# Hybrid attention and DeltaNet trunk: a quarter-size product in the second inversion level, and a later slot for layer 1's second query tile

## The chip, the cores and the metric

The kernel runs on one core of one Trainium2 chip. Its time is the device time of one execution in microseconds (us), as the median of the runs shown: 2465.13 us of 3 runs, from 2462.39 to 2465.59.

## The reference, cut to what matters

Two layers (DEPTH = 2) work on 512 tokens of 2048 channels: 256 context tokens and 256 latent ones. Each layer has one input projection, a mixer with two groups of 8 heads (group A is differential softmax attention, group B a bidirectional gated DeltaNet), and one output projection with an adaLN gate. Layer 1 doesn't update the context, so its attention has only latent queries. The parts that the change touches, shortened:

```python
def diff_attend(q, k, v, lam):                      # group A
    s = jnp.einsum('bhmqd,bhmkd->bhmqk', q, k) * (A_HEAD_DIM ** -0.5)
    p = jax.nn.softmax(s, axis=-1)
    a = p[:, :, 0] - lam * p[:, :, 1]
    return jnp.einsum('bhqk,bhkd->bhqd', a, v)

def gated_delta_chunked(q, k, v, g, beta, s0):      # group B, once forward, once flipped
    ...
    m = jnp.where(tri_strict, k_beta @ k.T * decay, 0.0) + jnp.eye(CHUNK)
    rhs = jnp.concatenate([v * beta[..., None], k_beta * jnp.exp(g)[..., None]], axis=-1)
    sol = lax.linalg.triangular_solve(m, rhs, left_side=True, lower=True, unit_diagonal=True)
    ...                                             # then a scan over the chunks
```

## The kernel before, in words

**Stages.** Each layer runs nine bodies, one after the other (`heads`). Body i projects head i's eight column tiles out of the 2048 channels and at the same time "fills" with the mixer of head i-1; body 0 only projects. The ninth (`project` is false) runs the mixer of head 7 beside the output projection. Body 0 of a layer, body 1 of layer 0 and the ninth are written out, the others run as a loop.

**Slots.** The order inside a body is written out by hand. It has 64 slots. Every engine (PE, DVE, ScalarE, and SP for the loads) builds a plan with `put(slot, function)` and then goes through the slots in order: first the slot's share of the projection, then the planned functions in the order in which they were put. On PE a slot of projection is six matmul rows of 128x512 (two k-tiles, each as hi x hi, L1808, hi weights x lo, L1809, lo weights x hi, L1810, since the float32 operands are split into a high and a low part); in layer 1 four of the eight tiles, the queries and the gates, are needed for the latent tokens alone and have half the width. On ScalarE a slot s with s % 4 = 1 begins with `split_hi` (L660, which waits for the weights' DMA), on DVE one with s % 4 = 2 with `split_lo` (L1113, `w_lo`). An engine that waits in a function holds up everything behind it on that engine.

**Solving the triangular system.** The kernel takes 128 tokens as one chunk (NT = 4 of them) and forms the inverse of the triangular matrix for both directions d, as `inv` and as its transpose `inv_T`. SP's `blocks_to_partitions` (L581 to L590) brings the 16x16 diagonal blocks onto partitions; DVE substitutes in four pieces (`substitute_backward`, slots 15 to 18 of layer 1, helpers at L296 and L312); SP's `blocks_back` (L592 to L601) stores the solution and issues eight DMAs (L600) that place the blocks into one of the two matrices; DVE's `turn_inv` (L1372, slots 24 and 25 of layer 1) transposes it into the other. Then the block size is doubled three times (`LEVELS = (16, 32, 64)`, so LVL = 3):
- levels n = 0 and 1, in layer 1 from slot 26 + 4n, in layer 0 from 23 + 4n, for each direction: `times_m` on PE (L1889, `m_T` x `inv` into bank GX[d]), `mask_x` on DVE (L1113 is the helper that records it, out of PSUM into `prod`), `times_inv` on PE (L1897 `inv_T` x `prod` into GX[d], L1898 `prod` x `inv_T` into GT[d], each for four chunks), and `merge` on DVE (two subtractions of 128x512, from `inv` and from `inv_T`; also recorded as L1113);
- the last level, the corners (slots 31 and 32 of layer 0, 34 and 35 of layer 1), in 64x64 pieces: `corner_times_m` (L1908) reads of `inv` only the quarter `QUAD[d]`, `copy_corners` (DVE, L1404), `corner_times_inv` (L1917) and `merge_corners` (two scalings of 64x256 out of PSUM, L1410). Behind it only `inv_T` is read (`v_mul`).

A float32 matmul has two rows in the trace for one call of `mm`, a 64x64 one too, so that four products stand as eight rows.

**Attention.** A query tile of 128 tokens goes through `score` on PE (L1985, 2 matmuls), `a_max` on DVE (L1470), `exps` on ScalarE (L929), `a_mix` on DVE (L1479 to L1482), `turn_p` on PE (L1992), `p_copy` on ScalarE (L941), `attend` on PE (L1999) and `oa_copy` on ScalarE (L946). Behind the last tile come `oa_squares` on ScalarE (L951), `oa_sums` on DVE (L1488), a power on POOL, `oa_norm` on DVE one slot ahead of `TURN_OA`, `turn_oa` on PE (L2005), and `y_out` on DVE and the store of y by ScalarE's DMA queue one and two slots behind it. `rotate` (PE, L2016) and `rope` (DVE, one slot later) turn the projected queries and keys of the next head; the first `rotate` of a body waits for `y_out`. The slots stand in tables (L456 to L470), with s for each entry of SCORE:

```python
SCORE, TURN_P, ATTEND = {0: (3, 11, 19, 27), 1: (4, 16)}, {0: 5, 1: 6}, {0: 7, 1: 8}
put(s, score, n); put(s + TURN_P[layer], turn_p, n); put(s + ATTEND[layer], attend, n)   # PE
put(s + 1, a_max, n); put(s + TURN_P[layer] - (3 if layer and n == 0 else 2), a_mix, n)  # DVE
put(SCORE[layer][-1] + ATTEND[layer] + 1, oa_sums); put(TURN_OA[layer] - 1, oa_norm)     # DVE
```

**adaLN.** The adaLN columns still wanted (in layer 1 its gate) are projected in the same bodies. In layer 1 PE multiplies at slots 10 and 16 (L1727, weights in `ada_raw` loaded by ScalarE's queue), behind `score` in slot 16; ScalarE copies the sum (L678, slot 17, behind `exps` of the same slot), and PE turns it in slot 18 (`ada_turn`, L1736), which waits for that copy.

The functions that the diff touches and what calls them:

Of the kernel before, what the change touches and what calls it, by code (L numbers as in the profile page):

```python
# [17 lines left out]
ALU = mybir.AluOpType  # L18
# [132 lines left out]
def build_trunk(nc, x, c, ctx_in, c_ctx, w_ada, b_ada, norm_w, w_in, conv_w, dn_a_log, dn_dt_bias,  # L151
# [15 lines left out]
    with ExitStack() as ctx:  # L167
# [52 lines left out]
        inv, inv_T, m_T = inv_m[:, 0:2], inv_m[:, 2:4], inv_m[:, 4:6]  # L220
        solved = inv_m[:, 1:3]
        m_turned, m_upper = inv_m[:, 3], inv_m[:, 3:5]
        prod = carve(2 * T).rearrange("p (x c d) -> p x c d", x=2, d=P)
# [42 lines left out]
        GX, GT = (G0, G2), (G1, G3)  # L266
# [60 lines left out]
        def quads(b):  # L327
            return ps[:, b, :].rearrange("p (c d) -> p c d", d=P)
# [126 lines left out]
        LVL = len(LEVELS)  # L455
        LEVELS_OF = (LVL, LVL - 1)  # L456
        WIDE = LEVELS[-1]
        QUAD = (slice(0, WIDE), slice(WIDE, 2 * WIDE))
# [2 lines left out]
        CORNERS = {0: 31, 1: 34}  # L461
        V_SLOT = {0: (35, 41, 47, 53), 1: (37, 43, 48, 54)}
        O_SLOT = {0: 56, 1: 57}
        SCORE, TURN_P, ATTEND = {0: (3, 11, 19, 27), 1: (4, 16)}, {0: 5, 1: 6}, {0: 7, 1: 8}
        TABLE_PE, TABLE_ACT = {0: (2, 5, 8), 1: (9, 16, 20)}, {0: (3, 6, 8), 1: (10, 17, 20)}
        TABLE_DVE = {0: (2, 4, 6, 8), 1: (9, 14, 16, 18)}
        TURN_OA = {0: 38, 1: 30}
        ROTATE = {0: (41, 43), 1: (34, 42)}
        ADA_SLOT, ADA_EARLY = {0: (8, 12, 16, 20, 46, 52), 1: (10, 16)}, {0: 4, 1: 2}
        BLOCKS_OUT, BLOCKS_BACK = {0: 7, 1: 7}, {0: 9, 1: 10}  # L470

# [636 lines left out]
        def _(vec):  # L1108
            own = Count(vec, vec_step)
            V = nc.vector  # L1110

            def tt(o, a, b, op):
                return V.tensor_tensor(o, a, b, op)  # L1113
# [102 lines left out]
            for layer in range(DEPTH):  # L1216
# [50 lines left out]
                def body(i, project, fill):  # L1267
# [125 lines left out]

                    def merge(d, n):
                        vec.wait_ge(t_product[d], h(-1, LEVELS_OF[d], n + 1))
                        own.go(tt(inv[:, d], inv[:, d], quads(GX[d]), ALU.subtract))
                        tt(inv_T[:, d], inv_T[:, d], quads(GT[d]), ALU.subtract).then_inc(t_merged[d], 1)
                        vec.wait_ge(t_merged[d], h(-1, LEVELS_OF[d], n + 1))
                        own.settle()
# [300 lines left out]
        def _(pe):  # L1700
            mm = nc.tensor.matmul
# [5 lines left out]
            for b in range(4):  # L1707
                last = turn(ps[:, A0, b * P:(b + 1) * P], rows_in[:, b], ident)
# [65 lines left out]
            for g in range(ADA_START // 4):  # L1774
                for pair in range(8):
# [3 lines left out]
                    for k in range(2):  # L1779
                        kt = 2 * pair + k  # L1780
                        j = kt % 4
                        last = mm(ps[32 * j:32 * j + 32, A0, :], c_T[:, kt, :], wide[:, k, :],
                                  start=kt < 4, stop=kt >= KT - 4)
# [6 lines left out]
                for b in range(4):  # L1790
                    last = mm(ps[:, A1, 2 * b:2 * b + 2], ada_wide[:, g % 2, b * P:(b + 1) * P], sel, start=True, stop=True)
# [4 lines left out]
            for layer in range(DEPTH):  # L1796
# [19 lines left out]
                for half in range(2):  # L1816
                    pe.wait_ge(w_split, base + half + (3 if layer else 1))
                    for k in range(HALF):
                        pe.wait_ge(h_ready, layer * KT + half * HALF + k + 1)
                        last = unit_piece(base + half, PJ, 0, half, [k])  # L1820
                        if k == HALF - 1:
                            last.then_inc(w_used, 1)
                        if layer:
                            before_last, last = unit_piece(base + 2 + half, PJ + 1, tokens(layer, 0), half, [k], both=True)
# [24 lines left out]
                def body(i, project, fill):  # L1849
# [42 lines left out]
                    def times_inv(d, n):  # L1892
                        pe.wait_ge(x_masked[d], h(-1, LEVELS_OF[d], n + 1))
                        if project and (d, n) == (0, 0):
                            pe.wait_ge(mod_ready, i * ADA_IN[layer] + (ada_before(layer) + ADA_EARLY[layer]))
                        for cc in range(NT):
                            mm(quads(GX[d])[:, cc], inv_T[:, d, cc], prod[:, d, cc], start=True, stop=True)  # L1897
                            last = mm(quads(GT[d])[:, cc], prod[:, d, cc], inv_T[:, d, cc], start=True, stop=True)  # L1898
                        last.then_inc(t_product[d], 1)

                    def corner_times_m():
# [193 lines left out]
                    for s in range(SLOTS):  # L2095
                        if project and not (layer and isinstance(i, int) and i == 0 and s < 2 * SLOTS // UNITS):
                            k = s // 4
                            t, half = k // 2, k % 2
                            if s % 4 == 0:
                                pe.wait_ge(w_split, i * UNITS + (base + 2 + k + 1))  # L2100
                                if half == 0:
                                    pe.wait_ge(evacuated, i * TILES + (layer * LAYER_TILES + 1 + t - 1))
                            last = unit_piece(base + 2 + k, PJ + (1 + t) % 2, tokens(layer, t), half,
                                              [2 * (s % 4), 2 * (s % 4) + 1])
# [61 lines left out]
```

## Time and profile before

| | before |
|---|---|
| median of 3 runs | 2465.13 us |
| lowest and highest | 2462.39, 2465.59 us |
| the profiled execution's own time | 2461.05 us |
| its span in the profile | 2459.3 us |
| mean granted clock of PE | 0.972 |
| PE busy | 2289.7 us, 93% |
| DVE busy | 1374.0 us, 56% |
| ScalarE busy | 918.7 us, 37% |
| POOL busy | 143.1 us, 6% |

The profile is of one execution. Its span runs from the first to the last recorded instruction, and the execution's own time is 1.75 us longer than it. PE means TensorE's matmuls, PEld its weight loads, ACT is ScalarE, SP SyncE, and a q behind a name (SPq) the engine's DMA queue. The granted clock is a share of TensorE's full rate. L1897 is line 1897 of the kernel, and where a helper records an operation the line is the helper's. Matmuls overlap each other in the records, so the distance between starts says more on a row's cost than its duration.

### The profile page before, as it was taken

Reading aid. Unit: us, or ns where it says so; the run is one execution under the profiler, and the core shown is the slowest. Engines: PE = TensorE matmul, PEld = TensorE weight load, DVE = VectorE, ACT = ScalarE, POOL = GpSimd, SP = SyncE. Lnnn points to the kernel's source line nnn. Section 1 sums busy time; section 2 is a strip of 40 time slices with the busy share of each in tenths; the row PEclk is TensorE's granted clock in tenths of the full one; section 3 lists DMA queues with packets and bytes.
Section 4 is the critical chain, followed back from the end, with each engine's and each line's share of the span. In section 5 each row is a group of like instructions: output and inputs, shape, how many; then the busy total and the mean of one; then the engine's idle time right before and its main releaser. Section 6 shows DMA issues by size and latency. Waiting matters only on the chain. (4 is left out here: it accounts for less than half of the span.)

```text
span 2459.3 us, 38535 instructions
## 1 busy us (share of the span) xinstructions
PE 2289.7 (93%) x13868; PEld 1852.7 (75%) x13868; DVE 1374.0 (56%) x2331; ACT 918.7 (37%) x1689; POOL 143.1 (6%) x183
## 2 busy tenths in 40 slices
PE   5789999999999999999999979899999999999887
PEld 3167787777778787878788758787887878787886
DVE  0334655546464646565654555656566565656665
ACT  3432424242433424242522363443424243342533
POOL 0000000000001000000100300000000000000002
PEclk8989999999999999999999989999999999999998
DMA  8974534243343435343545534433424343343554
GB/s 314 352 222 120 159 90 137 83 127 116 110 137 111 141 90 162 90 136 91 183 122 153 171 92 119 118 106 95 137 73 126 86 119 107 94 122 89 162 164 127
DMA packets 488882, 328.93 MB, mean 134 GB/s; under 512 B 48754, under 2 KB 452374, under 8 KB 488294
## 3 DMA queue, kind: packets, MB, share of 16 engines
q1 hardware_dynamic: 393750, 219.64, 31.6%
q10 hardware_dynamic: 94992, 108.09, 13.5%
q8 instruction: 46, 0.75, 0.1%
q14 instruction: 30, 0.25, 0.0%
q0 software_dynamic: 64, 0.20, 0.0%
HBM read 304.73 MB, written 23.13 MB: 133 GB/s over the span
## 5 line engine op out<-in xcount | busy, mean ns | idle before, releaser
L1808 PE MATMUL ps<-h_hi,w_hi 128*128 128x512 f32 (+1 forms) x2080 | 825.3, 397 | 18.1 <-DVE w_lo L1113 10.8
L1810 PE MATMUL ps<-h_hi,w_lo 128*128 128x512 f32 (+1 forms) x2080 | 768.1, 369 | 0.0
L1809 PE MATMUL ps<-h_lo,w_hi 128*128 128x512 f32 (+1 forms) x2080 | 767.6, 369 | 0.0
L1113 DVE TENSOR_TENSOR w_lo<-w_raw,w_hi 128x1024 fp32r<-128x1024 f32 (+1 forms) x300 | 365.4, 1218 | 290.6 <-ACT w_hi L660 251.4
L1808 PEld LDWEIGHTS ps<-h_hi,w_hi 128*128 128x128 f32 x2080 | 400.2, 192 | 125.3 <-issue 51.4
L660 ACT CAST w_hi<-w_raw 128x1024 fp32r<-128x1024 f32 (+1 forms) x300 | 311.5, 1038 | 369.5 <-PE ps L1810 188.0
L1810 PEld LDWEIGHTS ps<-h_hi,w_lo 128*128 128x128 f32 x2080 | 397.5, 191 | 68.5
L1809 PEld LDWEIGHTS ps<-h_lo,w_hi 128*128 128x128 f32 x2080 | 400.3, 192 | 49.8
L2089 PE MATMUL ps<-h_hi,w_hi 128*128 128x512 f32 (+1 forms) x448 | 157.8, 352 | 7.7 <-DVE h_lo L1113 6.6
L1648 POOL TENSOR_SCALAR small<-small 128x4 f32<-128x4 f32 (+3 forms) x51 | 20.5, 402 | 2254.5 <-DVE small L1488 987.4
L2090 PE MATMUL ps<-h_lo,w_hi 128*128 128x512 f32 (+1 forms) x448 | 151.7, 339 | 0.0
L2091 PE MATMUL ps<-h_hi,w_lo 128*128 128x512 f32 (+1 forms) x448 | 151.6, 338 | 0.0
L1113 DVE TENSOR_TENSOR arena<-arena,ps 128x512 f32<-128x512 f32 (+1 forms) x176 | 106.7, 636 | 61.5 <-PE ps L1898 58.5
L1288 DVE SCALAR_TENSOR_TENSOR arena<-arena,convh 128x512 f32<-128x512 f32 (+1 forms) x192 | 135.7, 707 | 7.0 <-DVE arena L312 1.1
L899 ACT ACTIVATE arena<-ps,hcol 128x128 f32<-128x128 f32 x128 | 40.1, 365 | 201.8 <-PE ps L1935 201.1
L1897 PE MATMUL ps<-arena 128*128 128x128 f32 x512 | 99.5, 276 | 8.2 <-DVE arena L1113 8.2
L2089 PEld LDWEIGHTS ps<-h_hi,w_hi 128*128 128x128 f32 x448 | 85.9, 192 | 20.6 <-issue 10.6
L1898 PE MATMUL ps<-arena 128*128 128x128 f32 x512 | 99.0, 275 | 0.0
L929 ACT ACTIVATE arena<-ps,small 128x512 f32<-128x512 f32 (+1 forms) x96 | 58.3, 612 | 101.4 <-DVE small L1471 99.0
L2091 PEld LDWEIGHTS ps<-h_hi,w_lo 128*128 128x128 f32 x448 | 85.7, 191 | 9.2
L2090 PEld LDWEIGHTS ps<-h_lo,w_hi 128*128 128x128 f32 x448 | 86.0, 192 | 7.7
L1897 PEld LDWEIGHTS ps<-arena 128*128 128x128 f32 x512 | 81.1, 191 | 13.4 <-DVE arena L1113 9.6
(199 smaller groups left out, 2769.7 us busy)
## 6 DMA issues: line engine op xcount, KB each, us to landing
w_raw<-in_w_in SPq DMA_DIRECT2D x260, 512.0 KB, 4.0
ada_raw<-in_w_ada ACTq DMA_DIRECT2D x128, 512.0 KB, 4.7
w_raw<-in_w_out SPq DMA_DIRECT2D x36, 448.0 KB, 3.8
arena<-in_w_ada SPq DMA_DIRECT2D x27, 512.0 KB, 8.4
arena<-in_w_out SPq DMA_DIRECT2D x28, 448.0 KB, 4.4
w_raw<-in_w_ada SPq DMA_DIRECT2D x19, 512.0 KB, 8.4
ada_raw<-in_w_ada SPq DMA_DIRECT2D x18, 512.0 KB, 8.3
arena<-decay_rows ACTq DMA_DIRECT2D x16, 512.0 KB, 6.2
```

The source lines that it names most:

```text
L660: nc.scalar.copy(w_hi[:, u % SPLIT, 0:tiles], raw_units[s][:, 0:tiles]).then_inc(w_hi_ready, 1)
L929: last = nc.scalar.activation(prob[:, m, 0:keys], bank(A0 + m, keys), ACT.Exp, scale=0.125, bias=small[:, 34 + m:35 + m], accum_out=small[ ...
L1113: return V.tensor_tensor(o, a, b, op)
L1288: m = V.scalar_tensor_tensor(acc, src, w, acc, ALU.mult, ALU.add)
L1808: mm(o, w_hi[:, s, k], h_hi[:, kt, t0:], start=kt == 0, stop=False)
L1809: before_last = mm(o, w_hi[:, s, k], h_lo[:, kt, t0:], start=False, stop=False)
L1810: last = mm(o, w_lo[:, s, k], h_hi[:, kt, t0:], start=False, stop=kt == KT - 1)
L1897: mm(quads(GX[d])[:, cc], inv_T[:, d, cc], prod[:, d, cc], start=True, stop=True)
L1898: last = mm(quads(GT[d])[:, cc], prod[:, d, cc], inv_T[:, d, cc], start=True, stop=True)
L2089: mm(o, w_hi[:, u % SPLIT, k], h_hi[:, kt, c0 * P:], start=kt == 0, stop=False)
L2090: mm(o, w_hi[:, u % SPLIT, k], h_lo[:, kt, c0 * P:], start=False, stop=False)
L2091: last = mm(o, w_lo[:, u % SPLIT, k], h_hi[:, kt, c0 * P:], start=False, stop=kt == HALF + OUT_HEADS - 1)
```

## The change

It has two parts.

In `times_inv`, the product into GT now comes ahead of the one into GX at both levels. At the second level (n = 1) the product into GX is formed only for rows and columns `QUAD[d]`, a 64x64 quarter of each chunk, and `merge` subtracts only that quarter from `inv`, 64x256 instead of 128x512. At the first level both stay full.

In layer 1, the second query tile's `score` goes from slot 16 to slot 25, and with it `a_max` from 17 to 26, `exps` from 17 to 26, `a_mix` from 20 to 29, `turn_p` and `p_copy` from 22 to 31, `attend` and `oa_copy` from 24 to 33, `oa_squares` and `oa_sums` from 25 to 34. `oa_norm` goes from 29 to 37, `turn_oa` from 30 to 38, `y_out` from 31 to 39, the store of y from 32 to 40. `rotate` goes from slots 34 and 42 to 41 and 43, and `rope` from 35 and 43 to 42 and 44. In the last body of layer 1 `y_lo_last` and `y_hi_last` of group A go from 32 to 40. In layer 0 the tables stay as they are.

```diff
@@ -461,11 +461,11 @@
         CORNERS = {0: 31, 1: 34}
         V_SLOT = {0: (35, 41, 47, 53), 1: (37, 43, 48, 54)}
         O_SLOT = {0: 56, 1: 57}
-        SCORE, TURN_P, ATTEND = {0: (3, 11, 19, 27), 1: (4, 16)}, {0: 5, 1: 6}, {0: 7, 1: 8}
+        SCORE, TURN_P, ATTEND = {0: (3, 11, 19, 27), 1: (4, 25)}, {0: 5, 1: 6}, {0: 7, 1: 8}
         TABLE_PE, TABLE_ACT = {0: (2, 5, 8), 1: (9, 16, 20)}, {0: (3, 6, 8), 1: (10, 17, 20)}
         TABLE_DVE = {0: (2, 4, 6, 8), 1: (9, 14, 16, 18)}
-        TURN_OA = {0: 38, 1: 30}
-        ROTATE = {0: (41, 43), 1: (34, 42)}
+        TURN_OA = {0: 38, 1: 38}
+        ROTATE = {0: (41, 43), 1: (41, 43)}
         ADA_SLOT, ADA_EARLY = {0: (8, 12, 16, 20, 46, 52), 1: (10, 16)}, {0: 4, 1: 2}
         BLOCKS_OUT, BLOCKS_BACK = {0: 7, 1: 7}, {0: 9, 1: 10}
 
@@ -1393,7 +1393,9 @@
 
                     def merge(d, n):
                         vec.wait_ge(t_product[d], h(-1, LEVELS_OF[d], n + 1))
-                        own.go(tt(inv[:, d], inv[:, d], quads(GX[d]), ALU.subtract))
+                        part, product = (inv[:, d], quads(GX[d])) if n < LVL - 2 else (
+                            inv[QUAD[d], d, :, QUAD[d]], quads(GX[d])[QUAD[d], :, QUAD[d]])
+                        own.go(tt(part, part, product, ALU.subtract))
                         tt(inv_T[:, d], inv_T[:, d], quads(GT[d]), ALU.subtract).then_inc(t_merged[d], 1)
                         vec.wait_ge(t_merged[d], h(-1, LEVELS_OF[d], n + 1))
                         own.settle()
@@ -1894,8 +1896,12 @@
                         if project and (d, n) == (0, 0):
                             pe.wait_ge(mod_ready, i * ADA_IN[layer] + (ada_before(layer) + ADA_EARLY[layer]))
                         for cc in range(NT):
-                            mm(quads(GX[d])[:, cc], inv_T[:, d, cc], prod[:, d, cc], start=True, stop=True)
                             last = mm(quads(GT[d])[:, cc], prod[:, d, cc], inv_T[:, d, cc], start=True, stop=True)
+                            if n < LVL - 2:
+                                last = mm(quads(GX[d])[:, cc], inv_T[:, d, cc], prod[:, d, cc], start=True, stop=True)
+                            else:
+                                last = mm(quads(GX[d])[QUAD[d], cc, QUAD[d]], inv_T[QUAD[d], d, cc, QUAD[d]],
+                                          prod[QUAD[d], d, cc, QUAD[d]], start=True, stop=True)
                         last.then_inc(t_product[d], 1)
 
                     def corner_times_m():
```

## Rows read from the trace of the kernel before

**Rows 1.** Page, section 1: busy us, share of the span, instructions of each engine.

```profile
PE 2289.7 (93%) x13868; PEld 1852.7 (75%) x13868; DVE 1374.0 (56%) x2331; ACT 918.7 (37%) x1689; POOL 143.1 (6%) x183
```

**Rows 2.** Waits of PE: line waited for, us in total, times, longest us.

```profile
PE ps L1736 <- ACT ada_sb L678: 21.3, 7, 4.0
...
PE ps L1908 <- issue: 9.5, 7, 1.4
```

**Rows 3.** Timeline, head 4 of layer 1: start, us, engine, operation [idle before <-releaser].

```profile
1887.24 1.13 PE L1985 MATMUL ps<-arena 64*128 64x512 f32 x4
...
1888.30 1.11 PE L1727 MATMUL ps<-ada_raw,c_T 128*32 128x256 f32 x16
...
1890.62 1.05 ACT L660 CAST w_hi<-w_raw 128x1024 fp32r<-128x1024 f32 x1 [4.28 <-DMA w_raw<-in_w_in]
...
1891.65 1.22 DVE L1470 TENSOR_REDUCE small<-ps 128x2 f32<-128x1024 f32 x1
...
1893.11 0.17 DVE L296 TENSOR_TENSOR arena<-arena 64x14 f32<-64x14 f32 x1
...
1894.86 0.37 ACT L678 COPY ada_sb<-ps 128x256 f32<-128x256 f32 x1 [0.29 <-ACT arena L929]
...
1895.28 1.01 PE L1736 MATMUL ps<-cst,ada_sb 128*128 128x2 f32 x4 [2.93 <-ACT ada_sb L678]
...
1899.16 0.19 DVE L312 TENSOR_SCALAR arena<-arena 64x64 f32<-64x64 f32 x1
...
1901.37 3.65 SPq L600 DMA_DIRECT2D arena<-s_blocks  x8
...
1906.61 1.46 DVE L1372 STREAM_TRANSPOSE arena<-arena 128x512 f32<-128x512 f32 x2
...
1910.50 0.42 DVE L1488 TENSOR_REDUCE small<-arena 128x2 f32<-128x256 f32 x1 [2.43 <-ACT arena L951]
...
1913.61 0.49 PE L1897 MATMUL ps<-arena 128*128 128x128 f32 x2 [1.17 <-DVE arena L1113]
```

**Rows 4.** Windows: stretch, us, busy of PE, PEld, DVE, ACT, POOL, clock, DMA, GB/s.

```profile
1895.90:1900.70 4.80, 4.80 (x13) 3.83 (x14) 4.28 (x7) 1.04 (x1) 0.00 (x0) 0.50 0.42 115
```

**Rows 5.** Lines by form: busy us, mean ns of one, idle before <-releaser.

```profile
L1897 PE MATMUL ps<-arena 128*128 128x128 f32 x512 | 99.5, 276 | 8.2 <-DVE arena L1113 8.2
...
L1113 DVE TENSOR_TENSOR arena<-arena,ps 128x512 f32<-128x512 f32 x144 | 93.2, 684 | 60.4 <-PE ps L1898 58.5 <-PE ps L1745 0.9
...
L1410 DVE TENSOR_SCALAR arena<-ps 64x256 f32<-64x256 f32 x32 | 13.5, 422 | 23.0 <-PE ps L1917 22.5
```

**Rows 6.** Timeline of PE, same head: a second-level call, then the corner.

```profile
1923.34 0.38 PE L1897 MATMUL ps<-arena 128*128 128x128 f32 x2
...
1929.98 0.68 PE L1908 MATMUL ps<-arena 64*64 64x64 f32 x16
```

**Rows 7.** Timeline of PE around the corner's second group, same head.

```profile
1932.28 0.39 PE L1810 MATMUL ps<-h_hi,w_lo 128*128 128x512 f32 x1
1932.60 0.68 PE L1917 MATMUL ps<-arena 64*64 64x64 f32 x16
...
1933.21 0.50 PE L1808 MATMUL ps<-h_hi,w_hi 128*128 128x512 f32 x1
1933.55 0.39 PE L1809 MATMUL ps<-h_lo,w_hi 128*128 128x512 f32 x1
```

**Rows 8.** Timeline, a head of layer 0 at its corner.

```profile
1134.15 1.28 DVE L1113 TENSOR_TENSOR arena<-arena,ps 128x512 f32<-128x512 f32 x2
...
1135.54 0.68 PE L1908 MATMUL ps<-arena 64*64 64x64 f32 x16 [1.39 <-issue]
```

**Rows 9.** Timeline, head 1 of layer 1 at the adaLN turn.

```profile
1564.88 1.04 ACT L660 CAST w_hi<-w_raw 128x1024 fp32r<-128x1024 f32 x1 [6.88 <-DMA w_raw<-in_w_in]
...
1567.99 1.01 PE L1736 MATMUL ps<-cst,ada_sb 128*128 128x2 f32 x4 [3.99 <-ACT ada_sb L678]
```

**Rows 10.** Timeline of PE, last body of layer 1.

```profile
2345.28 1.11 PE L1992 MATMUL ps<-cst,arena 128*128 128x128 f32 x4 [6.46 <-DVE arena L1482]
```

## The prediction

> **What bounds the kernel now.** I read the page first, then who waits for whom on PE, then the timeline of one head. PE is busy 93% of the span [rows 1]: inside the heads, whatever adds or removes PE time shows, unless a wait beside it absorbs it. PE's largest wait is the adaLN turn of L1736 for ScalarE's copy of L678: 21.3 us in 7 waits, one in each of layer 1's heads 1 to 7. The first corner product waits 7 times, 9.5 us, in layer 0 [rows 2].
>
> The first of these can be followed in head 4 of layer 1 [rows 3]. `score` of the second query tile runs at 1887.24 (slot 16). PE is through slot 18 at 1892.35 and waits 2.93 us. ScalarE's copy stands behind the exponentials of that tile, these behind DVE's maximum (1891.65), and that behind the substitution. Just behind the wait the granted clock is 0.50, the lower of PE's two levels (1.2 instead of 2.4 GHz) [rows 4].
>
> **The sum** is made against the profiled execution's own 2461.05 us, 4.08 below the median of 2465.13; the 4.08 is added at the end. A measurement of this kernel can tell about 0.2% (4.9 us) from no change.
>
> **Part 1, the quarter.** In `times_inv` at the second level (32 calls: 16 heads, two directions) four full GX products of two rows each become 64x64 ones. Today a call has 16 rows and takes 1.80 us, 0.112 a row: L1897's 512 rows are half of those of 64 calls [rows 5], and the call that starts at 1923.34 is one of them [rows 6]. With half the columns a row takes 0.056, so a call is 8 x 0.112 + 8 x 0.056 = 1.34 us, 0.46 less. But full and 64x64 products now alternate, and the array goes to the small form four times a call. What such a visit costs is seen at the corners [rows 7]: the group L1917 (16 rows) starts 0.32 us behind the last full row instead of 0.23, so 0.09 late, and from its start at 1932.60 to 1933.55 (the second full row behind it), less 0.23 for the first, are 0.72. Two quadrants at a time its work is 16 x 0.056 / 2 = 0.45, so the visit costs 0.09 + 0.27 = 0.36 us beyond its work. For a visit in `times_inv` the ends are 0 (everything hides under the next product) and 0.36. I take the late entry whole and two thirds of the rest, since the lone quadrant fills one set of weights and not two: 0.26 to 0.27. A call then takes 2.39, **0.59 longer**; by the ends 0.46 shorter or 0.98 longer.
>
> The Trainium skill speaks against this part: TensorEngine Tiling (Array Packing), Key Properties, says that a change of tiling mode drains TensorE, without a figure. The late entry of 0.09 agrees with it. [...]
>
> GT ahead of GX, at both levels, costs nothing: the wait stands ahead of both, and the same merge needs both. The shorter merge saves DVE 0.684 - 0.422 = 0.26 us a call, the second figure being a 64x256 write out of PSUM [rows 5].
>
> In layer 0, heads 1 to 7, PE waits 1.39 us at the corner for the merge of 1134.15 [rows 8]. Of the two calls only the first is in that DVE chain, and both merges are shorter: 0.59 - 0.52 = 0.07, times 7 = 0.5. PE's own 2 x 0.59 fills the wait that was there. The last head runs beside the output products without such a wait: 1.2. **Layer 0: 1.7 us slower.**
>
> **Part 2, head 4 of layer 1.** Ahead of slot 16 nothing moves. `score` leaves slot 16 (1888.30 - 1887.24 = 1.06 us), so PE reaches the turn at 1891.3. ScalarE's cast of w_hi waits for its DMA until 1890.62 and ends at 1891.67; the copy (0.37) now follows at once, and PE goes on at 1892.15 instead of 1895.28 [rows 3]. The wait shrinks from 2.93 to 0.85 us and the clock should stay up there.
>
> Then what is late next: at slot 26 PE needs `inv` turned. From 1892.15 it has the turn (0.4), slots 19 to 23 of six rows at 0.228 (6.85), three slots of half the width (2.1) and score (1.06): ready at 1902.6. The chain to it runs over DVE and SP: the substitution ends at 1899.35, eight DMA issues go out from 1901.37 to 1905.02, the transposition starts at 1906.61 [rows 3]. It gains only the DVE time that the maximum frees, 1891.65 to the next substitution row at 1893.11 and the gap ahead, 1.6 us. So the transposition (0.73 for the first direction) starts at 1905.0, times_m at 1905.75, and **PE idles about 3.1 us at slot 26**. The stall goes there, as long as those behind which the clock fell.
>
> Past it DVE is crowded. The 2.43 us wait of L1488 and the op leave slot 25, but the maximum (1.5) comes ahead of the first mask, and the mix (1.2) takes the place of oa_norm and y_out (0.9). The first times_inv comes at 1910.7 instead of 1913.61, behind a wait of 1.5 instead of 1.17, and the second level's at 1920.4 instead of 1923.34: 2.9 us ahead [rows 3, 6]. From there to the corner it was 6.64: two calls (3.6) and two slots of products. Now the calls take 4.78, and attend (8 rows, 0.85) lies between: 8.7, 2.0 longer. turn_oa (0.3) still has to come. What moves behind it I cost at nothing: the oa sum, POOL's power and oa_norm have slots 34 to 37 (three slots of 1.37), y_out is two slots ahead of the rotation that waits for it, and the ropes (three DVE ops each, slots 42 and 44) fit ahead of state(1) at 45, by under 0.5 us. The one DMA that moves, ScalarE's store of y, has the rest of the head to land in; SP's queue keeps its order, and POOL's next wait is at slot 59. **Net with the clock high: 2.9 - 2.0 - 0.3 = 0.6 us faster.**
>
> If the clock falls at slot 26, PE works at half speed for 3 to 7 us, but DVE sets the pace there and 1.5 us of PE wait can be used up. That costs between 0.1 and 1.4 us; I take 0.6, between the ends, since the fall can also be missed. Heads 2 to 7: 0 each.
>
> Head 1 [rows 9]: its turn came at 1567.99, but the cast ended only at 1565.92, so 1.6 us is won less 1.06 for score, the low clock stays, and the same cast holds DVE's chain. I estimate 1.3 at the first mask, less 2.3 behind it: 1.0 slower. The last body of layer 1 has one large wait, 6.46 us at turn_p behind substitution and mix [rows 10]. With turn_p away from slot 22 PE waits instead for product sums and then for the transposition; from head 4's steps I price it 2.0 faster (0 to 4), less 1.2 for part 1: 0.8 faster.
>
> **Sum:** 1.7 + 0 + 1.0 - 0.8 = 1.9 us slower: 2463.0, and 2467.0 against the median.
>
> **Rivals.**
> (1) *The visit hides.* A call is then 0.46 shorter, 1.05 better than forecast. That counts once in 7 heads of layer 0 and twice in 9 others: 25 x 1.05 = 26 us, 2441. For it: a full product's weights load under the product ahead. Against it: the 0.09 and 0.27 of the corner group. 0.20.
> (2) *The visit costs its full 0.36*, a call 0.39 more than forecast: 25 x 0.39 = 10 us, 2477. Its place is the second level of layer 1, where PE has no wait left that could absorb it; it decides from 0.29 us a visit on (0.12 a call, 3 us). For it: the full fp32 product behind a quadrant may have to load its weights uncovered. 0.24.
> (3) *The clock falls at slot 26 in all of heads 2 to 7, at its full price:* 6 x 0.8 = 5 us, 2472. For it: all seven waits at L1736 had it. 0.11.
> (4) *The waits shrink further*: under 2 us at slot 26, clock high, 1.3 us a head better: 2459. Against it: the DMA part of the chain is measured. 0.13.
> That the change does not do what it says I leave out: every moved step is read from the slot tables.
>
> **Numbers.** The forecast itself has 0.32. Faster by over 0.2% (below 2460.2): rival 1 and most of rival 4, 0.30. Slower: rivals 2 and 3 and a little of the forecast, 0.37. The rest, 0.33, is within. The range of 2446 to 2480 leaves out the larger part of rival 1 and the tail of rival 2; the likeliest case alone spans 2461 to 2470.
>
> **What the changed profile would show.** Right: calls of the second level of 2.3 to 2.5 us; the wait at L1736 under 1 us in heads 2 to 7; a new PE wait of about 3 us ahead of times_m, released by the transposition, and the low clock behind that one; a corner wait of 0.2 in layer 0; about 1.0 us for the two ops of a second-level merge. Wrong: calls of 1.4 us (rival 1) or 2.7 (rival 2), a corner wait of layer 0 still above 1, L1736 still above 2, or a PE wait at rope, rotation or state(1) in slots 41 to 45.

## The result

The changed kernel takes 2476.85 us in the median of 9 runs (2470.59 to 2481.95), the kernel before, measured again beside it, 2462.39 (9 runs, 2454.96 to 2465.59). The ratio is 1.0059 with a 95% interval of 1.0044 to 1.0073: **slower by 14.5 us**, where the forecast was 1.9 us slower and rival 2 twelve. The time lies inside the range of 2446 to 2480, close to its upper end, and beyond 2461 to 2470, the range of the likeliest case alone.

| | before | after |
|---|---|---|
| median of 9 runs | 2462.39 us | 2476.85 us |
| span of the profiled execution | 2459.3 us | 2470.0 us |
| mean granted clock of PE | 0.972 | 0.978 |

The profiled executions differ by 10.7 us, and the stretches below are of these two.

### The profile after

The page's first section, which answers to [rows 1], has 22 us more of PE, and DVE works less:

```profile
PE 2311.6 (94%) x13868; PEld 1852.5 (75%) x13868; DVE 1366.8 (55%) x2331; ACT 918.4 (37%) x1689; POOL 141.9 (6%) x183
```

The waits of PE (line waited for, us in total, times, longest) answer to [rows 2]. The lines from `merge` on have moved by two, from `times_inv` on by six: L1738 is the adaLN turn, L1891 `times_m`, L1931 the product with the state (`ks_mul`), L1914 the first corner product.

```profile
PE ps L1891 <- DVE arena L1372: 23.9, 11, 4.7
...
PE ps L1931 <- DVE arena L1427: 5.9, 7, 0.8
...
PE ps L1738 <- ACT ada_sb L678: 3.4, 1, 3.4
```

The wait at the turn is gone in six of seven heads. One for the transposition has come in its place, and a small one in seven heads that before did not have. L1914 does not wait any more.

One second-level call of head 4 of layer 1, in the timeline of PE, answers to the first of [rows 6]: L1899 is now `prod` x `inv_T` (full), L1903 the quarter.

```profile
1929.95 0.46 PE L1899 MATMUL ps<-arena 128*128 128x128 f32 x2
1930.34 0.32 PE L1903 MATMUL ps<-arena 64*64 64x64 f32 x2
1930.60 0.49 PE L1899 MATMUL ps<-arena 128*128 128x128 f32 x2
1931.01 0.33 PE L1903 MATMUL ps<-arena 64*64 64x64 f32 x2
...
1932.62 0.50 PE L1810 MATMUL ps<-h_hi,w_hi 128*128 128x512 f32 x1
1932.95 0.39 PE L1811 MATMUL ps<-h_lo,w_hi 128*128 128x512 f32 x1
```

From the first full row to the projection behind it the call has 2.67 us, against the 1.80 worked out from [rows 5]. One chunk takes 1930.60 to 1931.27, 0.67: the full pair 0.41 instead of 0.22, the small one 0.26. With the two small rows at 0.056 each, a visit (one change to the 64x64 form and back) costs 0.67 - 0.22 - 0.11 = **0.34 us** beyond its work. And the row behind the call is 0.33 behind its predecessor instead of 0.23, so a call is 0.97 longer than before.

The loads of the weights (PEld) show where those 0.34 us stand. In the same place before:

```profile
1923.45 0.30 PEld L1898 LDWEIGHTS ps<-arena 128*128 128x128 f32 x2
1923.56 0.39 PE L1898 MATMUL ps<-arena 128*128 128x128 f32 x2
```

and after:

```profile
1930.34 0.19 PEld L1903 LDWEIGHTS ps<-arena 64*64 64x64 f32 x2
1930.59 0.30 PEld L1899 LDWEIGHTS ps<-arena 128*128 128x128 f32 x2
```

Before, a load starts 0.11 us ahead of its row, under the row in front. At both changes of form it starts together with its row (1930.34 and 1930.60), so nothing of it is hidden. Row by row the trace has four gaps that are longer than the work alone: into the small form 0.20 instead of 0.11, between the two small rows 0.11 instead of 0.056, back to the full form 0.15 instead of 0.056, and behind the first full row 0.21 instead of 0.11. They add up to the 0.34. No run tells the uncovered load from another cost of the change of form.

The same head at the turn, at slot 26 and behind the corner, out of the timeline of all engines, with [idle before <-releaser], answers to [rows 3]:

```profile
1901.27 0.37 ACT L678 COPY ada_sb<-ps 128x256 f32<-128x256 f32 x1
...
1901.74 0.55 PE L1738 MATMUL ps<-cst,ada_sb 128*128 128x2 f32 x4
...
1902.16 0.48 PE L1810 MATMUL ps<-h_hi,w_hi 128*128 128x512 f32 x1
...
1914.39 1.46 DVE L1372 STREAM_TRANSPOSE arena<-arena 128x512 f32<-128x512 f32 x2 [2.51 <-DMA arena<-s_blocks]
...
1915.16 1.77 PE L1891 MATMUL ps<-arena 128*128 128x128 f32 x8 [2.55 <-DVE arena L1372]
...
1952.61 1.22 DVE L1113 TENSOR_TENSOR w_lo<-w_raw,w_hi 128x1024 fp32r<-128x1024 f32 x1 [1.72 <-ACT w_hi L660]
1953.75 0.42 DVE L1113 TENSOR_TENSOR ps<-ps,cst 128x256 f32<-128x256 f32 x1
...
1955.93 0.42 DVE L1113 TENSOR_TENSOR arena<-arena,ps 128x256 f32<-128x256 f32 x1
1956.39 0.61 DVE L1427 SCALAR_TENSOR_TENSOR arena<-arena,hcol,ps 128x128 f32<-128x128 f32 x2
...
1957.05 0.71 PE L1931 MATMUL ps<-arena 128*128 128x128 f32 x4 [0.84 <-DVE arena L1427]
```

PE no longer waits at the turn; it waits 2.55 us ahead of `times_m`, since the transposition itself waits for the blocks' DMA. Further on, the six rope operations (1953.75 to 1956.35) stand between a late `w_lo` and `state` (L1427), and PE waits 0.84 us for the latter.

The windows of that head (stretch, us, busy time and count of PE, PEld, DVE, ACT, POOL, granted clock, DMA share, GB/s) answer to [rows 4]:

```profile
1911.60:1915.10 3.50, 1.01 (x8) 0.77 (x6) 0.99 (x2) 0.89 (x1) 0.00 (x0) 1.00 0.22 35
1915.20:1918.60 3.40, 3.40 (x17) 3.40 (x18) 3.08 (x4) 0.00 (x0) 0.00 (x0) 0.55 0.45 127
1918.60:1922.00 3.40, 3.40 (x30) 3.32 (x29) 3.14 (x6) 2.49 (x5) 0.00 (x0) 0.95 0.58 154
```

The clock falls to its lower level behind the new wait, for 3.4 us. In the profile before it was low for 6.8 us behind the turn:

```profile
1895.10:1901.70 6.60, 6.42 (x18) 5.22 (x19) 5.79 (x12) 1.17 (x2) 0.00 (x0) 0.52 0.33 89
```

**Where the 10.7 us are.** The length of a body is the distance between the first transpositions of q and k (`turn_qk`) of two bodies. In layer 0 the way from `times_m` to the corner grows from 24.8 to 25.4 us in heads 2 to 6: two calls of 0.97, less the wait of 1.39 that stood there. Times seven that is 3.9, and the last head, beside the output products, has 1.85 more. In layer 1, head 1 is 2.6 us longer, heads 2 to 7 are 0.1 to 1.0 longer (2.6 together), the last 0.3 shorter. Together 10.7; the other stretches differ by some 2 us either way.

### The profile page after: what moved, and what is told of

It is laid out like the page before. It is cut to its first block and busy times, and to the rows that moved or that the text cites. A ratio compares the mean times of both kernels' runs of the same rounds, so it can differ in the third digit from the quotient of the medians.

```text
span 2470.0 us, 38515 instructions
## 1 busy us (share of the span) xinstructions
PE 2311.6 (94%) x13868; PEld 1852.5 (75%) x13868; DVE 1366.8 (55%) x2331; ACT 918.4 (37%) x1689; POOL 141.9 (6%) x183
## 5 line engine op out<-in xcount | busy, mean ns | idle before, releaser
L1113 DVE TENSOR_TENSOR arena<-arena,ps 128x512 f32<-128x512 f32 (+2 forms) x176 | 99.5, 587 | 80.5 <-PE ps L1903 58.2
L1899 PE MATMUL ps<-arena 128*128 128x128 f32 x512 | 109.9, 296 | 1.5 <-DVE arena L1113 1.4
L2095 PEld LDWEIGHTS ps<-h_hi,w_hi 128*128 128x128 f32 x448 | 85.3, 190 | 22.2 <-issue 10.6
L1891 PE MATMUL ps<-arena 128*128 128x128 f32 x512 | 76.7, 298 | 25.0 <-DVE arena L1372 23.9
L1891 PEld LDWEIGHTS ps<-arena 128*128 128x128 f32 x512 | 70.7, 209 | 32.9 <-DVE arena L1372 28.5
```

Of the source, the lines that this page charges most:

```text
L1891: last = mm(quads(GX[d])[:, cc], m_T[:, d, cc], inv[:, d, cc], start=True, stop=True)
L2095: mm(o, w_hi[:, u % SPLIT, k], h_hi[:, kt, c0 * P:], start=kt == 0, stop=False)
```

## The experiments

Each kernel ran in five rounds beside the kernel before. Two theories stood against each other first. V: the visits to the 64x64 form are the loss, the slots a gain. S: the moved slots are the loss.

### Part 1 alone

```diff
-        SCORE, TURN_P, ATTEND = {0: (3, 11, 19, 27), 1: (4, 25)}, {0: 5, 1: 6}, {0: 7, 1: 8}
+        SCORE, TURN_P, ATTEND = {0: (3, 11, 19, 27), 1: (4, 16)}, {0: 5, 1: 6}, {0: 7, 1: 8}
 ...
-        TURN_OA = {0: 38, 1: 38}
-        ROTATE = {0: (41, 43), 1: (41, 43)}
+        TURN_OA = {0: 38, 1: 30}
+        ROTATE = {0: (41, 43), 1: (34, 42)}
```

(against the changed kernel). 

> The first part without the second: the quarter product, slot tables as before. Theory V (the visits to the 64x64 form are the loss): a second-level call takes 2.67 us as in the trace of the change, against 1.80, and delays the row behind it by another 0.1. In layer 0 the corner's wait of 1.39 takes up part: 0.6 a head in seven heads and 1.9 in the last, 6 us. In layer 1 nothing takes it up: 1.9 in each of eight heads, 15.5 us. Together 21 us slower, ratio to before 1.0088 (1.006 to 1.011). Theory S (the moved slots are the loss): only layer 0's 6 us, ratio 1.0025, at most 1.004.

Measured: 1.0056 (1.0037 to 1.0075). That is above the 1.0025 of theory S, whose upper end of 1.004 the interval just touches, and a little below theory V's range of 1.006 to 1.011. The way from the first `times_m` of a body to its corner, which has no low clock in either profile, is longer by 1.6 us in heads 2 to 7 of layer 1 (22.5 instead of 20.9) and by 19 us in all sixteen bodies together, near theory V's 21. But the seven turn waits of its profile are all followed by 3.4 us of low clock and not by 6.8, which the sum had not foreseen, and so its bodies of heads 2 to 7, 108.9 to 109.6 us, are no longer than before. What the clock is worth is seen below.

### Part 2 alone

The change's three table lines on the kernel before. 

> The second part without the first: score of the second query tile in slot 25 and what hangs on it, full products. Theory V: the change's 14.5 us less part 1's 21: 7 us faster than before, ratio 0.997 (0.994 to 0.999), the loop's heads of layer 1 about 1 to 1.5 us shorter than before. Theory S: slower, the change's 14.5 less layer 0's 6, ratio 1.003. Under both the wait at the adaLN turn is gone and about 2.6 us stand ahead of the first times_m of layer 1 instead.

Measured: 0.9978 (0.9966 to 0.9989), as theory V had it. The loop's bodies of layer 1 have 107.6 to 107.9 us from head 3 on, against 109.0 to 109.5 before. So **the second part by itself is a gain of some 5 us, and the first a loss of some 14**. Together they should give 1.0034; measured is 1.0059. The three intervals allow it, so the runs do not show whether the two parts get in each other's way.

### One visit a call, and two

```diff
                         for cc in range(NT):
                             last = mm(quads(GT[d])[:, cc], prod[:, d, cc], inv_T[:, d, cc], start=True, stop=True)
                             if n < LVL - 2:
                                 last = mm(quads(GX[d])[:, cc], inv_T[:, d, cc], prod[:, d, cc], start=True, stop=True)
-                            else:
-                                last = mm(quads(GX[d])[QUAD[d], cc, QUAD[d]], ...)
+                        for cc in range(NT if n == LVL - 2 else 0):
+                            last = mm(quads(GX[d])[QUAD[d], cc, QUAD[d]], ...)
```

(the slots as before; the kernel with two visits does the same for two chunks at a time). 

> Part 1 alone with another order at the second level: the four full products into GT first, then the four 64x64 ones together, so one visit to the small form a call instead of four. Theory V1 (what costs is the visit, 0.33 us beyond its rows at 0.056 each): 8 full rows at 0.112, 8 small at 0.056 and one visit: 1.7 us a call against 1.80 before and 2.67 with four visits, so the time within 0.2% of before, ratio 0.998 to 1.001. Theory V2 (rows in one and the same quadrant are no faster than full ones, 0.107, and the visit itself costs about 0.2): 1.95 us a call, 0.15 to 0.25 more than before, ratio 1.001 to 1.003.

> Part 1 alone with two visits a call (two full products into GT, two small ones, twice). Theory V: the cost goes with the number of visits: calls of 1.59 with one and 2.67 with four give 0.36 a visit, so 1.95 us here, and the ratio lies between 0.9957 (one) and 1.0056 (four) on the same line, 0.9990 (0.997 to 1.001). Rival (only the last small product or the alternation of single products hurts, not the count): a call within 0.1 of 1.59 or of 2.67.

Measured: 0.9957 (0.994 to 0.9974) with one visit, 0.9997 (0.9984 to 1.0011) with two, beside 1.0056 with four. The timeline of PE with one visit:

```profile
1922.48 1.05 PE L1899 MATMUL ps<-arena 128*128 128x128 f32 x8
1923.47 0.67 PE L1903 MATMUL ps<-arena 64*64 64x64 f32 x8
1924.07 0.50 PE L1810 MATMUL ps<-h_hi,w_hi 128*128 128x512 f32 x1
1924.41 0.39 PE L1811 MATMUL ps<-h_lo,w_hi 128*128 128x512 f32 x1
```

and with two:

```profile
1925.98 0.61 PE L1900 MATMUL ps<-arena 128*128 128x128 f32 x4
1926.52 0.44 PE L1904 MATMUL ps<-arena 64*64 64x64 f32 x4
1926.89 0.71 PE L1900 MATMUL ps<-arena 128*128 128x128 f32 x4
1927.54 0.44 PE L1904 MATMUL ps<-arena 64*64 64x64 f32 x4
1927.91 0.50 PE L1810 MATMUL ps<-h_hi,w_hi 128*128 128x512 f32 x1
```

The same 16 rows take 1.59 us with one visit, 1.93 with two, 2.67 with four: 0.34 for the second, 0.37 for each of the other two. The cost goes by the number of visits, and V2 (small rows at 0.107) falls, since eight of them with the way back take 0.60. The time with one visit was missed: its calls are 0.2 us shorter (0.1 with the late row behind), some 3 us in all, and it gained about 10. In layer 0 the corner comes 0.5 us sooner a head. Over all sixteen bodies the way from `times_m` to the corner is 7 us shorter than before, in layer 0 by more than the calls alone, which fits the shorter merges. The other 3 us are inside the interval and have no shown cause; the low clock can be part of them (below).

### The narrow product without a visit

```diff
+                                last = mm(quads(GX[d])[:, cc, QUAD[d]], inv_T[:, d, cc], prod[:, d, cc, QUAD[d]], ...)
```

(all 128 rows of `inv_T` as weights, 64 moving columns, the quarter's rows used; slots as before). 

> Part 1 alone without any visit: the product stays in the form of 128x128 weights and only its moving columns are cut from 128 to 64; the merge is the quarter. Theory N1 (a row's spacing follows its columns): 8 rows at 0.112 and 8 at 0.056, 1.35 us a call, 0.45 less in each of 32 calls, some of it waiting in layer 0: 10 us faster, ratio 0.996. Theory N2 (a float32 row with a full set of weights takes 0.112 whatever its columns, as L1736's rows of two columns have 0.112 from start to start in the trace of before): 1.80 us a call as before; only the shorter merges are left, at most 0.5 us a head in layer 0 where the corner waits for them, ratio 0.998 to 1.000.

Measured: 0.9974 (0.9961 to 0.9987). One chunk and the next in its timeline of PE:

```profile
1917.01 0.44 PE L1899 MATMUL ps<-arena 128*128 128x128 f32 x2
1917.29 0.33 PE L1903 MATMUL ps<-arena 128*128 128x64 f32 x2
1917.45 0.44 PE L1899 MATMUL ps<-arena 128*128 128x128 f32 x2
```

The full pair has 0.28 and the narrow one 0.16, 0.44 a chunk where two full pairs have 0.45; the call takes 1.70. Half the columns save almost nothing, so N2 holds for the call. The time came out a little below its bound.

### The order alone

```diff
-                            mm(quads(GX[d])[:, cc], inv_T[:, d, cc], prod[:, d, cc], start=True, stop=True)
-                            last = mm(quads(GT[d])[:, cc], prod[:, d, cc], inv_T[:, d, cc], start=True, stop=True)
+                            mm(quads(GT[d])[:, cc], prod[:, d, cc], inv_T[:, d, cc], start=True, stop=True)
+                            last = mm(quads(GX[d])[:, cc], inv_T[:, d, cc], prod[:, d, cc], start=True, stop=True)
```

> Only the order of the two products is changed, GT ahead of GX, at both levels, both full, merges full. The prediction costed it at nothing: ratio 1.000 (0.9985 to 1.0015), a second-level call 1.80 us as before. Rival (the order carries part of the loss of part 1): ratio above 1.0015, a longer first merge or a longer call.

Measured: 1.001 (0.9993 to 1.0026). No difference that can be told from none. Its profile shows something else: with the slots of before, head 4 has a body of 109.0 us, and head 2 one of 107.3. The windows behind their turns differ (columns as above, head 2 first):

```profile
1683.00:1686.00 3.00, 3.00 (x8) 2.32 (x9) 2.90 (x4) 0.25 (x1) 0.00 (x0) 0.50 0.55 148
1686.20:1689.40 3.20, 3.20 (x15) 2.65 (x15) 2.49 (x8) 0.60 (x1) 0.00 (x0) 1.00 0.11 28
...
1897.60:1904.30 6.70, 6.55 (x18) 5.30 (x19) 5.89 (x12) 1.14 (x2) 0.00 (x0) 0.52 0.32 88
```

Their waits at the turn were alike, 2.28 and 2.48 us. With 6.8 us of low clock the body of head 4 is 1.7 us longer than that of head 2 with 3.4; over heads 2 to 7 of this profile such differences are 0.9 to 2.0. So one and the same kernel has both lengths in one execution; the profile before had 6.8 in all seven heads, that of part 1 alone 3.4 in all seven, that with one visit 3.4 in three.

### Idle rows in the two waits

```diff
+                    def spin(rows):
+                        for r in range(rows):
+                            mm(bank(G1), h_hi[:, r, 0:P], h_hi[:, r, 0:T], start=True, stop=True)
...
+                        if layer and fill:
+                            need(pe, mod_ready, i * ADA_IN[layer] + (ada_before(layer) + k + 1) - 2)
+                            spin(8)
                         ada_turn(...)
```

(the kernel before; in the second kernel, with part 2's slots, eight such rows into the bank GX[0] stand ahead of the first `times_m`, without the line of `need`). 

> The kernel before, with eight idle matmul rows of 128x512 (1.8 us of PE work whose result nobody reads) ahead of the adaLN turn in layer 1's bodies 1 to 7, inside the wait of 2.7 to 4.0 us, so that PE stays at work where it stood still. Theory C (the low clock behind the wait costs about 1.9 us a head, the difference between heads with 6.8 us of it and heads with 3.4 in the profile with one visit): no low clock behind the turn in most heads, each some 2 us shorter, 13 us faster, ratio 0.995. Rival (DVE sets the pace and the low clock is absorbed): heads as long as before, ratio 0.9995 to 1.001.

> The second part alone, with eight such idle rows (1.8 us) ahead of the wait for the transposition in slot 26 (2.6 us). Theory C: the low clock behind slot 26 is gone and each head is 0.6 us or more shorter than with part 2 alone: ratio to before 0.9955 to 0.997. Rival (DVE sets the pace there: in the profile of part 2 alone heads with the low clock behind slot 26 and without it were equally long, 107.6 and 107.7): the low clock goes, the time stays at 0.9978, a PE wait of 1.5 at the first times_inv takes its place.

Measured: 0.9981 (0.9967 to 0.9995) at the turn, 0.9988 (0.9977 to 0.9998) at slot 26. Timeline and window with the rows at the turn:

```profile
1890.24 1.98 PE L2031 MATMUL ps<-h_hi 128*128 128x512 f32 x8
...
1892.87 0.61 PE L1736 MATMUL ps<-cst,ada_sb 128*128 128x2 f32 x4 [0.66 <-ACT ada_sb L678]
```

```profile
1892.90:1899.60 6.70, 6.17 (x28) 4.85 (x28) 5.89 (x12) 1.06 (x1) 0.00 (x0) 1.00 0.31 88
```

The clock stays at its upper level in all of layer 1's loop, and the bodies of heads 2 to 7 have 106.9 to 107.5 us, 1.5 to 2.3 less than in the profile before. So the low clock behind the turn does cost time. The ratio is worth only 4.7 us of the 13 expected. One reason is on record: the profile before, with its seven long stretches, has a mean granted clock of 0.972, while the 81 executions of the kernel before that ran beside these experiments have 0.974 in the mean, so many of them have less low clock to lose. With the idle rows it is 0.980.

At slot 26 the low clock goes as well, and nothing is won over part 2 alone (0.9978). In the kernel with part 2 alone, head 3 had no low clock and head 4 had 3.4 us of it (PE's timeline, head 3 first):

```profile
1804.38 1.16 PE L1889 MATMUL ps<-arena 128*128 128x128 f32 x8 [2.68 <-DVE arena L1372]
...
1809.31 0.49 PE L1897 MATMUL ps<-arena 128*128 128x128 f32 x2 [1.46 <-DVE arena L1113]
...
1911.93 1.53 PE L1889 MATMUL ps<-arena 128*128 128x128 f32 x8 [2.66 <-DVE arena L1372]
```

Head 3 waits 1.46 us at the first `times_inv` for DVE, head 4, whose products ran at the lower clock, not at all; their bodies have 107.7 and 107.6 us. DVE sets the pace there, and a fall of 3.4 us is paid out of that wait. A longer one is not, as the next profile shows.

### The ropes behind `state`

```diff
-        ROTATE = {0: (41, 43), 1: (41, 43)}
+        ROTATE = {0: (41, 43), 1: (41, 46)}
```

(part 2 alone otherwise). 

> The second part alone, but the second rotation in slot 46 and its rope in 47, behind state(1) in slot 45, instead of 43 and 44 ahead of it. Theory R (two ropes and a late w_lo in slots 42 to 44 hold up state(1), and PE's new wait of 0.84 at ks_mul is their price): the wait is gone, each of eight heads of layer 1 0.8 us shorter than with part 2 alone, ratio to before 0.9978 less 0.0027: 0.9951 (0.993 to 0.997). Rival (the wait moves to the next product, or into the corner of the next head): heads as with part 2 alone, 107.6, ratio 0.9978.

Measured: 0.9956 (0.9939 to 0.9973). The wait of 0.84 at `ks_mul` is gone from the waits of PE, and the way from the corner's second group to the end of the body has 38.8 us instead of 39.6 in heads 1 to 7 of layer 1. Theory R holds; part 2's own slots leave 0.8 us a head behind.

Two heads of this profile, 3 and 5, have 6.8 us of low clock behind slot 26. The window of head 3 (columns as above):

```profile
1792.10:1798.90 6.80, 6.15 (x29) 6.15 (x30) 6.22 (x9) 1.82 (x5) 0.00 (x0) 0.50 0.53 147
```

Their way from `times_m` to the corner has 23.2 and 23.0 us, and that of heads 2, 4, 6 and 7, with 3.4 us of low clock, 22.2. So behind slot 26 the short stretch costs nothing and the long one 0.8 to 1.0 us.

### Combinations

> The whole change, but with the four small products of a call together, one visit to the 64x64 form instead of four. Theory V (four visits a call are the loss, the slots are a small gain): the two single results multiply, 0.9957 x 0.9978 = 0.9935, 16 us faster than before; a second-level call 1.6 us. Rival (the two gains are one and the same, both get rid of time behind PE's wait and the low clock of layer 1): ratio 0.995 to 0.997, no better than the one visit alone.

Measured: 0.9952 (0.9935 to 0.997). That is inside the rival's 0.995 to 0.997, while the product of 0.9935 stands at the very edge of the interval.

> One visit a call, the second part's slots, and the second rope in slot 47. Theory R: 0.8 us a head off the kernel with one visit and part 2 (0.9952): ratio 0.9925 (0.991 to 0.994), the fastest of all, heads of layer 1 at 106.7. Rival: no better than 0.9952.

Measured: 0.9946 (0.9927 to 0.9964), in the profile with bodies of 106.6 to 106.9 us in heads 3 to 7 and of 108.0 in head 2. The expected 0.9925 (0.991 to 0.994) was missed.

> One visit a call, slots as before, and eight idle matmul rows ahead of layer 1's adaLN turn. If the two gains are independent, 0.9957 x 0.9981 = 0.9938. If the one visit's gain beyond its 0.2 us a call (0.9957 where its calls give about 0.998) is itself that fewer heads run through a long stretch of low clock, the idle rows add nothing to it: 0.9955 to 0.997.

Measured: 0.9945 (0.9924 to 0.9966). The expected product 0.9938 and the rival's 0.9955 are both in the interval; it does not decide.

One visit with part 2 and the later rope takes 2444.33 us in the median, **16 us less than before** (2460.34 beside it; the ratio is worth 13) and, by the two ratios, some 28 less than the changed kernel. It cannot be told from the kernel with the idle rows (2446.82) or the one without the later rope (2446.72).

## Why the prediction was right, and where it was not

**The forecast itself was missed, and it is partly luck where the time landed.** The time is inside the range because the range was kept wide for rival 2. It meets that rival's 2477 almost to the figure, though the rival counted from 2465.13, the median of three, and measured beside it the kernel before has 2462.39. Nor do the two parts have their prices. The sum makes part 1 11.3 us slower (1.7 in layer 0 and 1.2 in each of eight heads), 21 with rival 2's price, and part 2 by itself 9.4 faster; measured are some 14 and 5.

**What bounds the kernel** was right: PE's added time shows wherever no wait beside it absorbs it, and the two waits named moved as described.

**Part 1: the term that was mis-sized is the visit.** The prediction took "the late entry whole and two thirds of the rest", 0.26 to 0.27 us, "since the lone quadrant fills one set of weights and not two". The changed trace has 0.34, near the 0.36 of the corner group [rows 7]. The two thirds were a guess with no row behind it, and the row was there. A second-level call grew by 0.97 (2.67 with 0.10 behind it) and not by 0.59. That is rival 2, whose price of 10 us on top of the forecast gives 12; its place, the second level of layer 1, was right as well. The count of visits was shown by one, two and four of them. The rule of the Trainium skill that a change of tiling mode drains TensorE (TensorEngine Tiling (Array Packing), Key Properties) pointed the right way, and these runs put 0.34 to 0.37 us on it. Rival 2's ground, weights that load uncovered behind a quadrant, is what the changed trace shows.

Rival 1 could have been weakened from rows as well. The adaLN turn has four rows of only two columns. At the upper clock the later ones of them start 0.112 us apart in the trace before, and in the changed one the four take 1902.16 - 1901.74 = 0.42 us, 0.105 each: a float32 row with full weights is hardly cheaper for having fewer columns. The narrow product showed the same, 0.44 a chunk against 0.45. The Trainium skill (TensorE: Matmul & The Clock Gate, Back-to-back issue gap) gives a gap by the columns alone only for a matmul by itself, and says that in a stream of weight loads and matmuls both set the spacing. The equal 0.11 us of 2, 64 and 128 columns agrees with the second and not with the first.

**Layer 0**: forecast 1.7, measured 3.9 and 1.85. The corner's wait of 1.39 was used up, as said, but whole, since two calls bring 1.94 and not 1.18; then PE and no longer DVE's chain sets the corner. The last head has nearly both calls, as said.

**GT ahead of GX** cost nothing that can be told from none (1.001, 0.9993 to 1.0026), as said.

**Part 2** came out in the profiles by errors that offset each other. The forecast of 0 for heads 2 to 7 had part 1's 1.2 in it, so it made part 2 by itself 1.2 us a head faster; the profile of part 2 alone has 1.4 against the one before. But that one has the long stretch of low clock in all of these heads, and heads with a short one and the slots of before (the order alone) have 107.3 to 108.1 us, much like the 107.6 to 108.3 of part 2 (the mean of its six heads is 107.8). Of its steps:
- The wait at slot 26 was forecast at about 3.1 us and is 2.55; the turn waits not at all instead of 0.85. `times_m` comes 3.9 us earlier in the body than before.
- The low clock behind slot 26 was priced at 0.6, between 0.1 and 1.4. It costs nothing where it lasts 3.4 us, as in all of these heads of the changed profile, and 0.8 to 1.0 where it lasts 6.8, as in two heads with the later rope. DVE sets the pace there, as the prediction said. Rival 3, the fall in all heads at 0.8 more each, had the fall right and the price not.
- "What moves behind it I cost at nothing" failed: "the ropes fit ahead of state(1) at 45, by under 0.5 us" left out that the `w_lo` of slot 42 waits for ScalarE's cast until 1952.61. The price is 0.84 us a head, and moving the rope took it away.

**Heads 2 to 7**: forecast 0 each, measured 0.43 on average. **Head 1**: 1.0, measured 2.6; its turn still waits 3.4 us, and the call's extra comes on top. **The last body**: 0.8 faster, measured 0.3, with the wait of 4.7 us at the transposition in place of 6.46 at `turn_p`.

**The clock before** was the blind spot, and the step that no row of one profile could show. The prediction took the profile's seven stretches as the kernel's, and they are the long ones; other heads of equal slots have the short one, and those of the order alone and of one visit are 1.0 to 2.0 us shorter for it. In the profile of part 2 alone even three heads of layer 0, whose slots it leaves as they are, have 3.4 us of low clock and bodies 1.5 to 2.7 us longer than before. Why a stretch is long or short with nearly the same wait ahead of it was not settled. Over the 81 executions of the kernel before, the time is some 1.5 us shorter for each 0.001 of mean granted clock. By that estimate the clock gave the kernels with four visits about 3.4 us back (0.976 in the mean of their executions, against 0.974), so that their products cost more than the ratios say: 19 - 3.4 is near part 1's 14. With one visit it was 0.975, which is worth at most 2 of the 10 us. It is likely also part of why the medians differ by 14.5 us and the profiles by 10.7: the profiled execution after has 0.978, above its kernel's mean, and the one before 0.972, below it.

## What to carry to other kernels

A smaller product is not a cheaper one where its rows have another array form than their neighbours: count the changes of form, and put all the small products of a group together, one visit for all. If a row for the unknown cost stands in the trace, take its value whole rather than a fraction argued from how the engine might work. And when a step is moved onto slots of another engine, look at how late that engine's own unplanned work runs there, not only at its share of the slot.

## What was unexpected of the hardware

A visit of TensorE to the 64x64 form costs 0.34 to 0.37 us, three full float32 rows' worth. The full pair behind one takes 0.41 us instead of 0.22. A float32 row with 128x128 weights takes 0.112 us with 128 columns, and full and 64-column pairs in turn take 0.44 us, 0.11 a row, as well. At a change of form the load of the weights starts with its row and not 0.11 us ahead of it. Behind waits of 2.3 to 2.5 us the clock was low for 3.4 us in some heads and 6.8 in others of one execution, and behind waits of 2.7 to 2.8 us in part 2 alone it did not fall in three heads. Eight idle rows (1.8 us) in the wait kept it high in all heads.
